# A Trainium2 decoder-layer kernel: the rows of the second norm's gain and bias built by TensorE instead of loaded

## What is computed

```python
x = layer_norm(ALPHA * x + token_mixer(x, ...), ln1_g, ln1_b)
x = layer_norm(ALPHA * x + peer(x, w_q, sub_keys, u, v), ln2_g, ln2_b)
x = x + sigmoid(x @ ple_w_gate) * (p @ ple_w_proj)

def peer_block(xb):                       # 128 tokens
    ...                                   # 8 heads choose 16 of 16384 experts for each token
    h = gelu(einsum('thkd,td->thk', u[eidx], xb))
    return einsum('thk,thkd->td', softmax(top) * h, v[eidx])
```

## Time and profile before

| what | value |
|---|---|
| median of 3 runs | 1782.41 us |
| profiled execution, its own time | 1783.08 us |
| its span, first to last instruction | 1781.1 us |
| TensorE busy (matmul) | 1574.5 us, 88% |
| VectorE busy | 1315.0 us, 74% |
| ScalarE busy | 777.8 us, 44% |
| GpSimd busy | 502.2 us, 28% |
| moved by DMA | 655.39 MB, of it 536.90 MB by the 512 gathers |
| mean granted clock of TensorE | 0.984 of full |

### The profile page before, as it was taken

The page is one execution under the profiler, slowest core; times in us unless marked ns, Lnnn a source line. Parts: engine busy times, 40 slices in busy tenths (PEclk is TensorE's granted clock), DMA queues, the critical chain, the costliest instruction groups (busy, mean ns, idle before and its releaser), DMA issues. The chain is left out here.

```text
span 1781.1 us, 16905 instructions
## 1 busy us (share of the span) xinstructions
PE 1574.5 (88%) x5000; PEld 873.9 (49%) x5000; DVE 1315.0 (74%) x2711; ACT 777.8 (44%) x1937; POOL 502.2 (28%) x528
## 2 busy tenths in 40 slices
PE   8999999999999997989788668888889878787788
PEld 7888888766655575545344222332333223222224
DVE  4454588699888999678878876876666677766676
ACT  6666695422222224343334334444444443444453
POOL 0000000122222232324343443433333343333341
PEclk9999999999999999999999989999999999999999
DMA  5113289799999999999999999999999999999994
GB/s 213 66 65 141 98 323 397 285 420 420 390 420 421 421 410 405 423 415 412 421 415 422 422 422 421 421 420 422 422 421 421 421 396 423 421 421 422 421 416 183
DMA packets 94932, 655.39 MB, mean 368 GB/s; under 512 B 10368, under 2 KB 14208, under 8 KB 17152
## 3 DMA queue, kind: packets, MB, share of 16 engines
q0 software_dynamic: 73728, 536.90, 72.8%
q1 hardware_dynamic: 20832, 116.97, 16.7%
q10 hardware_dynamic: 288, 0.52, 0.1%
HBM read 652.26 MB, written 2.10 MB: 367 GB/s over the span
## 5 line engine op out<-in xcount | busy, mean ns | idle before, releaser
L2107 PE MATMUL psum<-uv,diag 128*128 128x512 f32 x1424 | 709.0, 627 | 190.6 <-ACT diag L991 187.1
L720 POOL DMA_INDIRECT uv<-in_pk_uv,idx x512 | 499.8, 976 | 1244.0 <-PE psum L2107 562.9
L1592 DVE CUSTOM_DVE_ANT_0 uv<-uv,psum 128x1024 f32<-128x1024 f32 x512 | 623.2, 1218 | 299.5 <-DMA uv<-in_pk_uv,idx 292.3
L2107 PEld LDWEIGHTS psum<-uv,diag 128*128 128x128 f32 x1424 | 257.2, 194 | 611.8 <-ACT diag L991 391.2
L979 ACT ACTIVATE gelu<-dots 128x1 f32<-128x1 f32 x512 | 103.4, 202 | 757.1 <-DVE dots L1592 755.1
L2007 PE MATMUL psum<-xT,raw 128*128 128x384 f32 x640 | 208.4, 486 | 0.0
L1605 DVE SCALAR_TENSOR_TENSOR oT<-uv,coef,oT 128x1024 f32<-128x1024 f32 x151 | 193.4, 1281 | 6.2 <-ACT coef L983 6.2
L2007 PEld LDWEIGHTS psum<-xT,raw 128*128 128x128 f32 x640 | 120.7, 190 | 81.7
L983 ACT ACTIVATE coef<-gelu,weight 128x1 f32<-128x1 f32 x512 | 150.8, 295 | 16.6
L991 ACT ACTIVATE diag<-ident,coef 128x128 f32<-128x128 f32 x356 | 143.0, 402 | 11.6
L1843 PE MATMUL psum<-xTh,w_hi 128*128 128x512 f32 x248 | 98.8, 398 | 0.1
(11 more groups left out here) (281 smaller groups left out, 1709.8 us busy)
## 6 DMA issues: line engine op xcount, KB each, us to landing
raw<-in_w_in SPq DMA_DIRECT2D x32, 1024.0 KB, 8.9
raw_a<-in_w_a SPq DMA_DIRECT2D x12, 1024.0 KB, 4.7
raw<-in_pk_w_q SPq DMA_DIRECT2D x10, 1024.0 KB, 9.3
raw_y<-in_w_in SPq DMA_DIRECT2D x8, 1024.0 KB, 6.7
raw<-in_w_branch_a SPq DMA_DIRECT2D x8, 1024.0 KB, 7.4
uv<-in_pk_uv,idx POOLq DMA_INDIRECT x512, 15.2
raw<-in_w_out SPq DMA_DIRECT2D x6, 1024.0 KB, 12.0
raw_w<-in_pk_w_q SPq DMA_DIRECT2D x6, 1024.0 KB, 10.3
```

The costliest lines, as they stand in the source:

```text
L720: pool.indirect_dma_start(row_uv(r)[:], None, pk_uv, bass.IndirectOffsetOnAxis(idx[:, i % 2, j:j + 1], 0)).then_inc(row_loaded(r)[0], 16)
L1592: V.tensor_tensor_reduce(u, u, x_cur[:], 1.0, 0.0, ALU.mult, ALU.add, dots[:, r % 32:r % 32 + 1]).then_inc(dot_done, 1)
L2107: last = T.matmul(B[i][:], diag[:, n % DR, :], row_uv(r)[:, D + i * 512:D + (i + 1) * 512], start=(r in FIRST), stop=last_of_block, skip_g ...
```

## The change

The two loads, their two kernel inputs and SP's wait for `acc_out` go. A new TensorE step, `ln2_row(w)`, runs behind the other work of rows 124 (w = 0, gain) and 129 (w = 1, bias): for each half of the row it multiplies, four times, a column of `vecs`, spread over 128 columns as the stationary operand, by the identity, which puts 128 values of the vector on all 128 partitions, into bank 6 or 7. ScalarE copies each half (128x512) to the old place, `ln2_out(w)`, behind its work of rows 125 and 130; the bias halves wait for `acc_out`. The readers wait for counts of copies instead of loads, and `x2_turn(0)`, which uses banks 6 and 7 next, waits for the bias halves to be copied out.

```diff
--- before.py
+++ after.py
@@ -31,7 +31,7 @@
 
 
 def build(nc, x, x_t, p_t, w_a, w_in, vec_cols, w_branch_a, w_branch_b, w_out,
-          ln1_g, ln1_b, pk_w_q, sub_keys_t, pk_uv, ln2_g, ln2_b, ple_w_gate, ple_w_proj, out):
+          ln1_g, ln1_b, pk_w_q, sub_keys_t, pk_uv, ple_w_gate, ple_w_proj, out):
     SEQ, D = x.shape[1], x.shape[2]
     TB = SEQ // P
     KT = D // P
@@ -257,6 +257,7 @@
         ln_step, ln_var, ln_root, ln_rec = sem("ln_step"), sem("ln_var"), sem("ln_root"), sem("ln_rec")
         x1_done = sem("x1_done")
         x1n_done, x1T_step = sem("x1n_done"), sem("x1T_step")
+        ln2_mm = sem("ln2_mm")
         x1_cur = sem("x1_cur")
         row_in = [sem(f"row_in{i}") for i in range(len(o_uv))]
         dot_done, gelu_done, coef_done = sem("dot_done"), sem("gelu_done"), sem("coef_done")
@@ -378,6 +379,7 @@
         P_BANK = (6, 4)
         LAST_PARTS = [(0, 512), (512, 768), (768, 1024)]
         LAST_BANK = (2, 3, 0)
+        LN2_ROW = [BLOCK_ROWS - 4, BLOCK_ROWS + 1]
         C_ROW = [2 * BLOCK_ROWS + 46 + 2 * n for n in range(4 * KT)]
         X1_ROW = BLOCK_ROWS * (TB - 1) + 36
         HI_ROW = [ROWS - 18 + n for n in range(KT)]
@@ -609,10 +611,7 @@
 
             def first_parts(n):
 
-                if n < TB:
-                    sp.dma_start(x_of(n), xf[:, n, :]).then_inc(x_in[n], 16)
-                else:
-                    sp.dma_start(ln2_gain[:], ln2_g[0].partition_broadcast(P)).then_inc(ln2_in, 16)
+                sp.dma_start(x_of(n), xf[:, n, :]).then_inc(x_in[n], 16)
 
             for n in range(4, len(UNITS) // 2):
                 if n == 4:
@@ -624,7 +623,7 @@
                 unit_fetch(n)
                 if n == X_UNIT:
                     sp.wait_ge(t_done, USE["query", 0, PKH - 1, 1] + 1)
-                if X_UNIT <= n < X_UNIT + TB:
+                if X_UNIT <= n < X_UNIT + TB - 1:
                     first_parts(n - X_UNIT + 1)
 
             def tail_fetch(m, src, *name):
@@ -666,8 +665,6 @@
             query_fetch(3)
             load_p(0)
 
-            sp.wait_ge(acc_out, 2)
-            sp.dma_start(ln2_bias[:], ln2_b[0].partition_broadcast(P)).then_inc(ln2_in, 16)
             query_fetch(4)
             query_fetch(5)
             query_fetch(6)
@@ -1011,6 +1008,13 @@
                             query_out(1, h, [a])
                     if r == SCORE_ROW[h] + 1:
                         query_out(1, h, [2, 3])
+
+            def ln2_out(w):
+                for i in range(2):
+                    act.wait_ge(ln2_mm, 2 * w + i + 1)
+                    if w == 1:
+                        act.wait_ge(acc_out, i + 1)
+                    nc.scalar.activation(ln2[w][:, i * HW:(i + 1) * HW], B[6 + i][:], ACT.Copy).then_inc(ln2_in, 1)
 
             def x2_turn_out(b):
                 for kh in range(2):
@@ -1076,6 +1080,8 @@
                     if k == FIN_GATE[-1] + 1:
                         gate_tanh(b, 0)
                         gate_tanh(b, 1)
+                if r - 1 in LN2_ROW:
+                    ln2_out(LN2_ROW.index(r - 1))
                 if r in C_ROW and C_ROW.index(r) % KT == KT - 1:
                     c_copy(C_ROW.index(r) // KT)
                 if r in HI_ROW:
@@ -1622,12 +1628,12 @@
 
             def fin_scale(b):
                 if b == 0:
-                    dve.wait_ge(ln2_in, 16)
+                    dve.wait_ge(ln2_in, 2)
                 norm_scale(b, x2[:], x2[:], ln2[0], x2_step, x2_var)
 
             def fin_shift(b):
                 if b == 0:
-                    dve.wait_ge(ln2_in, 32)
+                    dve.wait_ge(ln2_in, 4)
                 norm_rstd(b, x2_root, x2_rec)
                 norm_shift(b, x2[:], ln2[1], x2_step, x2_rec, x2_done)
 
@@ -2116,6 +2122,19 @@
                     T.matmul(B[i][:].rearrange("p (k t) -> p k t", t=P), ident[:], acc[:, 4 * i:4 * i + 4, :],
                              start=False, stop=False, skip_group_check=True)
 
+            def ln2_row(w):
+
+                for i in range(2):
+                    if w == 0:
+                        pe.wait_ge(*t_reader(last_in(6 + i)))
+                    else:
+                        pe.wait_ge(ln2_in, i + 1)
+                    for k in range(4):
+                        col = (GAIN, BIAS)[w] + 4 * i + k
+                        last = T.matmul(B[6 + i][:, k * P:(k + 1) * P], vecs[:, col:col + 1].to_broadcast([P, P]), ident[:],
+                                        start=True, stop=True, skip_group_check=True)
+                    last.then_inc(ln2_mm, 1)
+
             def x2_turn(b):
                 for kh in range(2):
                     if b < TB - 1:
@@ -2125,7 +2144,7 @@
                     if b == 2:
                         pe.wait_ge(c_out, 4)
                     if b == 0:
-                        pe.wait_ge(*t_reader(last_in(6 + kh)))
+                        pe.wait_ge(ln2_in, 3 + kh)
                     else:
                         pe.wait_ge(fin_step, 2 * b)
                     for k in range(4):
@@ -2261,6 +2280,8 @@
                         gate_mm(b, FIN_GATE.index(k))
                     if k in FIN_P:
                         proj_mm(b, FIN_P.index(k))
+                if r in LN2_ROW:
+                    ln2_row(LN2_ROW.index(r))
                 if r in C_ROW:
                     c_matmul(C_ROW.index(r))
                 if r == ROWS - 8:
@@ -2321,8 +2342,6 @@
         "pk_w_q": _chunks(given["pk_w_q"][0]),
         "sub_keys_t": given["pk_sub_keys"][0].reshape(-1, *given["pk_sub_keys"].shape[3:]).transpose(2, 0, 1),
         "pk_uv": _np.concatenate([given["pk_u"][0], given["pk_v"][0]], axis=1),
-        "ln2_g": given["ln2_g"],
-        "ln2_b": given["ln2_b"],
         "ple_w_gate": _rows(given["ple_w_gate"][0]),
         "ple_w_proj": _rows(given["ple_w_proj"][0]),
     }
```

## The result

The changed kernel takes **1785.76 us** in the median of 22 runs (1784.39 to 1789.13), the kernel before 1782.40 in 22 runs beside them (1781.29 to 1785.29): +3.4 us, ratio 1.002 (95% interval 1.0013 to 1.0026). 1783.7 was forecast, within 1779.6 to 1787.4, and "no difference" up to 3.6 us, which it just is. The interval leaves out zero, so the kernel is slower by a little, and +3.4 is more than the +0.5 to +2.9 that the forecast gave to its own mechanism. The profiled execution took 1787.22 us, 1.5 above its median.

A forecast was written before the change was run, and what follows sets the result against it. DMA, gathering rows at 421 GB/s, bounds three quarters of the span, TensorE close behind. Loads 0, calls and copies +2.9 at row 131, clock giving back 0.8 and 1.3, row 139 +1.3: 1782.41 + 1.3 = 1783.7 us, range 1779.6 to 1787.4.

The forecast's parts named there:

- its own mechanism: Change of block: TensorE's calls and ScalarE's copies delay gathers, DMA carries +1.3 us to the end; bounds +0.5 to +2.9; 0.45.
- The loads are worth nothing: Gain load (490.04) and bias load (787.13): removing them taken as 0, of at most 1.25 and 1.8 us.
- The gain's mechanism: After the gain load's place: the shorter queue only empties earlier, at 700 to 715 us; issues of rows 104 to 108 decide.
- SP's wait releases nothing: SP's 31.6 us wait ended at 787; the query block 4 fetch behind it has its own wait, so nothing issues early.
- TensorE's calls: Rows 124 and 129: 16 instructions, 1.8 us a call; row 130's sum +3.6, second call hidden before row 131's sum.
- rival B: Matmuls paced by weight loads, 3.6 us a call: row 137 lands +5, 1787.4 us, slower; chance 0.18.
- ScalarE's copies: Some 1.1 us a pair: first hidden in row 125, second on the path at row 130, +1.1 before row 131's diagonal.
- The clock stayed up: Before row 131's sum: idle 1.4 us instead of 1.94, so clock stays at its upper level, giving back 0.8 and 1.3 us.
- The sum: Row 137's gather +2.1, landing at 809.4; row 139 lands at 814.3 instead of 813.00, +1.3 us carried to the end.
- Rival C: Behind row 133: TensorE's slack and the missing bias load absorb the shift to within 0.5 us, 1782.4 us; chance 0.18.
- A: Whole stream: every byte counts, 1.05 MB less gives 2.5 us, 3.1 with the poor rate; 1779.9 us, faster; chance 0.15.
- D: Block 0's norm 2: built rows come too late and it waits some microseconds for them, +2 to +4; chance 0.04.

The follow-up runs named there:

- both: Kernel before with both loads kept and the change's two TensorE calls and four ScalarE copies added, copies going to an unused tile: 1785.89 us against 1782.62.
- no_bias: Kernel before without the bias load and SP's wait alone, norm 2 reading block 3's x as bias: 1782.27 us against 1783.13.
- none: Kernel before without both loads and SP's wait, nothing in their place (norm 2 reads block 3's x): 1783.88 us against 1782.62.
- none2: The same kernel as none, run again in another group of runs: 1782.38 us against 1783.23 for the kernel before.
- gain119: Changed kernel with TensorE's first call at row 119 instead of 124, copied at row 120; second call still at row 129: 1784.89 us against 1783.13 before.
- mm_early: Changed kernel with TensorE's calls at rows 119 and 121, gain copied at row 120, bias still at row 130: 1785.15 us against 1782.62 before.
- no_gain: Kernel before without the gain load alone, norm 2 reading block 3's x as gain: 1782.91 us against 1783.13.
- all_early: As mm_early, with the bias copied at row 128 already: 1784.02 us against 1782.62 before; run again, 1784.57 against 1783.23.
- split_early: all_early with w_gate's 4 MB load cut into three: 1784.05 us against 1783.23 for the kernel before.
- split_before: Kernel before with w_gate's 4 MB load cut into three, the later parts behind the fetches of query blocks 2 and 3: 1783.70 us against 1783.13.
- bias130: Changed kernel with TensorE's second call at row 130 instead of 129 and its copies at row 131: 1786.71 us against 1783.23 before.

## Why the prediction was right, and where its sum was off

*The loads are worth nothing: right as far as it can be seen.* both and changed lie 0.1 us apart by their distances to before, where each interval is 3 us wide. The gain's mechanism is the one forecast (the head start is made and dies); only it dies earlier, between rows 70 and 78, by some 623 us, not at 700 to 715 us. The 0.55 us that the forecast gave to the bias load for its poor rate is not borne out: without that load no_bias moves 390 GB/s from 785 to 795 us, with it before moves 398. The forecast said dot products 109 to 123 within 0.3 us of before; in the changed kernel's profile most were 1 to 2 us late instead, in that of none 2.5; in the other profiles with the 4 MB load whole they kept their row 100's distance within 0.8 us, row 108 itself aside. none and none2 are one kernel and differ in this, so I put it down to the execution. That the load has a part in it is not ruled out: in the three profiles with the gain's load and the 4 MB whole (before, both, no_bias) it doesn't happen.

*SP's wait releases nothing: right.* The fetch behind it follows row 130's query matmuls in every run.

*TensorE's calls: right.* 1.79 us each for 1.8; rival B, 3.6, is out.

*ScalarE's copies: right.* 1.06 for 1.1, on the path, between root and table load. Their share of the loss is not shown by itself, as said above.

*The clock stayed up: right,* but behind 1.12 us of idle time, a little under the 1.2 to 1.6 of the forecast. (1.94 - 3.6 + 2.9 gives 1.24; the forecast's 1.4 took too early an end for the query matmuls.) What the forecast read out of it was not sound: that the clock comes back as a gain of 0.8 + 1.3 us. It holds against the one profile of before, in which the clock fell. The idle 1.94 us does not decide that, as six of nine profiles show, and in an execution of before in which the clock stayed up there is nothing to give back. How often that is among the timed runs, no trace tells.

*The sum: its last step was too small.* "Row 137: +2.1, so its row lands at 809.4", "+1.3 us" from row 139 on. Measured against row 124's own delay, row 137's gather was +2.2 late, as forecast, but its row +3.7 and row 139 +3.4; at row 145 the loss is 2.9. I had given row 137 the 6.5 us of the trace before, reading that nothing was ahead of it. That reading was wrong: row 136 and the fetch, 2.1 MB, had been issued 5.1 and 4.7 us earlier (795.68, 796.08), and the engines went on at 417 GB/s from 800.74 to 805.00 us. Now the row took 8.1 us from issue to dot product, and 7.9 and 8.3 in the two other runs with a second call at row 129 (both, gain119). In these three row 137's gather comes 3.75 us behind row 136's, before it was 5.07: row 136, the fetch and row 137, 3.1 MB, crowd within 4 us of each other, behind a hole. In the other runs the distance is 4.6 to 6.4 us, and the row takes 5.7 to 7.6 (mm_early, no_bias, no_gain, all_early twice, none, none2, split_early). split_before with 8.8 and bias130 with 8.9 do not fit: in the first the engines are full throughout (420 GB/s from 785 to 795 us), in the second VectorE is late. I had written the fetch down as late ("becoming about 798.8") and left its 1.05 MB out of DMA's order. That the crowding, or the fetch in it, is what delays row 137 is argued from these times; no run moved it alone.

The same loss can be booked as what DMA doesn't move. From row 124's dot product to row 160's before takes 100.5 us for 41.64 MB, which at 421.3 GB/s are 98.8: 1.6 us are missing. The changed kernel takes 103.3 us for 40.77 MB: 6.6 are missing. 5.0 more, less the bias load's 1.25, makes 3.7, while the stretch is 2.9 longer; the 0.8 between them I take for what was in flight at its ends.

*So the range held, and in part by luck.* Its upper end, 1787.4, is rival B's, which did not happen. The forecast's own mechanism is the one that the traces show, but its bounds of +0.5 to +2.9 missed the median's +3.4.

*Rival C* (absorbed) is out for the changed kernel; *A* is out; *D* did not happen: VectorE waited 0.75 us for the bias copies and not at all for the gain's.

What stays open: 1 to 2 us in the medians of mm_early and all_early that no profile of theirs shows; and whether a change of 1 us can be shown in this kernel at all, where the same kernel gave +1.3 and -0.9.

## What to carry to other kernels

In a kernel bound by DMA, bytes taken off have a price only where DMA sets the pace from there to the end. Find the next stretch in which another engine is busy without a gap, or in which DMA runs dry; here the saving was lost there. Work of 1.8 us on an engine with 12% of free time cost 1.5 us where this engine had no gap and releases buffers. Read the engine's own timeline row by row and put such work behind one of its waits. Where something becomes late, list every transfer that is issued around it, with its bytes, before giving any of them a latency from the old trace, and look at what the DMA engines were still moving there. And before a distance between two profiles is given to a change, look at the granted clock in both: here one and the same kernel differed by 1.8 us at the change of block in two profiles, one with a fallen clock and one without.

## What the runs showed that I had not expected

A stretch in which one engine is busy without a gap works one way: head starts of 2 to 4 us (row 60) were gone to within 0.04 us at row 78, while lateness passed the change of block in full. A head start that comes from putting bytes off is paid back as they are moved (split_before: 8 us at row 113, none at row 124). The clock can fall or stay behind the same idle time: of nine profiles with 1.94 us it fell in three. And one execution differs from the next in where a single gather lands beside a 4 MB load: row 108 waited for in one profile (727.47), row 109 in others (728.40 before), which moved the stream by up to 2.5 us.
